# Issuing the attention bias loads of pairs 1 to 3 from SyncE, ahead of the pair's weight units

## The chip, the cores and the metric
The kernel runs on one core of a Trainium2 chip, as one program. The metric is the device time of the whole program in microseconds (us), the median of several executions. TensorE multiplies (PE in the profile; PEld is its weight load), VectorE is DVE, ScalarE is ACT, GpSimd is POOL, and SyncE (SP) only issues DMAs. ScalarE issues DMAs too; in the profile the rows marked SPq and ACTq are issues of these two engines' queues.

## The reference
One inference step of a one-layer hybrid encoder in float32: 1024 prompt frames and 8 streams of 16 frames (T = 1152 token columns) with D_MODEL = 1024. The layer is a half-step SwiGLU FFN, then two token mixers side by side (chunk-band softmax attention and a gated delta rule), cross-attention to 256 memory tokens, a second half-step FFN and a final norm. What matters here is mixer A:

```python
def band_attention_prompt(q, k, v, table):          # 8 heads x 64
    bias = rel_bias(table, qrel[:, None] - krel[None, :])
    ...
        sc = jnp.einsum('bqhd,bkhd->bhqk', qc, kb).astype(jnp.float32) * scale + bias
        p = jax.nn.softmax(sc, axis=-1).astype(v.dtype)
        return jnp.einsum('bhqk,bkhd->bqhd', p, vb)
```

Queries see a band of nine chunks of 64 frames. The 8 running streams do the same against 512 cached keys and their own 16. Each head has its own bias, a function of the relative distance.

## The kernel before
All products with weights are made as three float32r products (high by high, low by high, high by low): a weight unit of 128 x 1024 is loaded raw, GpSimd splits it into `w_hi` and `w_lo` (L133 and L136, in `split_units`), and TensorE runs jobs of 24 matmuls with it (three jobs to a unit, one for each third of the 1152 tokens). Three raw slots and three split slots form a ring, so that a unit's load waits until the unit before it in its slot has been split (`unit_split`), and a split waits until the products of the unit before it in its slot are done (`dense_done`) and its own unit has landed (`raw_landed`).

Mixer A works by pairs of heads, four pairs of them (`PAIRS = 4`, numbered 0 to 3). Pair 0 uses seven units, each later pair six: units 0 and 1 give q and k at the start of the pair (jobs 3 to 8), units 2 to 5 are filler work spread by a fixed plan between the attention steps; units 2 to 4 feed the convolution of mixer B, and unit 5 gives v of the next pair. A pair has nine attention steps (eight tiles of 128 queries and the streams): scores on TensorE, bias add and maximum on VectorE, exponential on ScalarE, normalisation on VectorE, transposes and the product with v on TensorE. Each product with v (`values`, L1431, for the streams L1418) raises the semaphore `valued`. It starts with one token, so that `valued.at(9 * i + 1)` is reached when all nine steps of the pairs before pair i have their values. After the ninth, TensorE runs only the last 16 filler matmuls of its pair before job 3 of the next one; job 3 needs that pair's unit 0 split (`job`, `n == 0`).

Every engine's instructions are in program order. TensorE, in a later pair: job 3, the transposes of v (`turn_v`, L1474 and L1477), jobs 4 to 7, the first scores, job 8, then the nine steps. There are two PSUM banks for jobs, so job 5 waits until ScalarE has evacuated job 3 (`take`, L1570). ScalarE, at the turn from one pair to the next: the last evacuation of v (L1528), the store of the pair's output (`ya`, L1657), `load_bias(i)` (L1557 to L1566), `next_conv` and `load_conv` (four DMA issues, L1545 to L1555), `take` of job 3, the copy of v, and the loads of the key and value caches (L1578), 2048 KB each.

`load_bias(i)` loads what pair i adds to its scores: for each of the two heads one window of 128 x 640 values (320 KB) and four copies of 16 x 528 values (33 KB), ten DMAs and 904 KB in all. VectorE waits for them (`a_loaded`) before it masks two corners of `bias` (L1726 and L1727) and adds it in its first step (L1740).

SyncE's queue in this stage is `load_units` (L71 to L108). It is called for pair 0 with one turn of seven units, and at its end loads the first three units of pair 1 ahead (L108). It is then called for pairs 1 to 3 with `turns = 3` and `turn = 6`: turn 0 (pair 1) issues its units 3 to 5; a hardware loop takes turn 1 (pair 2), and turn 2 (pair 3) is written out, both with units 0 to 5 (L82). `load_units` has a hook, `at_turn`, that is called once in each turn: in turn 0 behind the place of unit 0, in the later turns ahead of unit 0. The kernel before doesn't use it in this stage.

Of the kernel before, what the change touches and what calls it, by code (L numbers as in the profile page):

```python
# [17 lines left out]
DB, DS = 8, 16  # L18
# [5 lines left out]
HA, DHA, REACH, REL = 8, 64, 512, 128  # L24
HB, DHB, CW = 4, 128, 4
HX, DHX, NMEM = 4, 256, 256
WIN = REACH + P
# [27 lines left out]
def slot(j, turn):  # L55

    if (j, turn) == (4, 5):
        return 2
    return 1 if turn % RING == 1 and j == turn - 1 else j % RING


def sharing(j, turn):

    return [u for u in range(turn) if slot(u, turn) == slot(j, turn)]


def last_use(j, turn):

    same = sharing(j, turn)
    at = same.index(j)  # L70
    return (0, same[at - 1]) if at else (1, same[-1])  # L71


def load_units(sp, k, first, turns, turn, at_turn=None, then=None, apart=0, last=True):

    def one(i, j):
        back, last = last_use(j, turn)
        if not (isinstance(i, int) and i < back):  # L80
            sp.wait_ge(k.unit_split.sem, k.unit_split.at(turn * i + (last + 1 - turn * back)))
        sp.dma_start(k.w_raw[slot(j, turn)][:, :], k.units[k.host_unit(k.phase, i, first, j)])\  # L82
            .then_inc(k.raw_landed[slot(j, turn)].sem, 16)
    for j in range(turn):
        if j >= k.ahead:
            one(0, j)
        if at_turn and j == 0:
            at_turn(0)
        if then and j == RING - 1:
            then()  # L90
    if turns > 1:
        with sp.Fori(1, turns - apart) as i:
            if at_turn:
                at_turn(i)
            for j in range(turn):
                one(i, j)
    for i in range(turns - apart, turns):
        if at_turn:
            at_turn(i)
        for j in range(turn):  # L100
            one(i, j)
    if not last:
        return
    k.ahead = units_ahead(k)
    for j in range(k.ahead):
        users = sharing(j, turn) or [turn - 1]
        sp.wait_ge(k.unit_split.sem, k.unit_split.at(turn * (turns - 1) + users[-1] + 1))
        sp.dma_start(k.w_raw[j][:, :], k.units[k.host_unit(k.phase + 1, 0, first + turns * turn, j)]).then_inc(k.raw_landed[j].sem, 16)  # L108


def units_ahead(k):

    return min(RING, k.turn_sizes[k.phase + 1]) if k.phase + 1 < len(k.turn_sizes) else 0
# [59 lines left out]
def units_done(k, turns, turn):  # L173

    for u in range(turn):
        k.raw_landed[slot(u, turn)].base += 16 * turns
    for sig in (k.unit_hi, k.unit_split):
        sig.base += turns * turn
    k.next_unit += turns * turn
    k.phase += 1  # L180
# [1097 lines left out]
def attention_phase(nc, k, norm, decay, head, xh, xl, x, x_to, work):  # L1278
# [3 lines left out]
    def sb(name, shape):  # L1282
        t = nc.alloc_sbuf_tensor_at(name, shape, F32, offset=at[0])
        at[0] += (4 * int(np.prod(shape[1:])) + 31) // 32 * 32
        return t
# [7 lines left out]
    bias, bias_s = sb("a_bias", [P, 2, WIN]), sb("a_bias_s", [P, REACH + DS])  # L1293
# [6 lines left out]
    PAIRS, ND = HA // 2, 2  # L1300
# [8 lines left out]
    STEPS, SAMPLE, FULL = len(TILES), TILES.index(None), 4  # L1309
# [16 lines left out]
    shifted = k.bias_dram_flat[P - 1:P - 1 + P * (k.bias_pitch - 1)].rearrange("(q m) -> q m", q=P)[:, 0:HA * NBIAS]\  # L1326
        .rearrange("q (h m) -> h q m", h=HA)

    def window(t):

        n = min(5, t + 1)
        return t + 1 - n, n

    def keys_of(s):

        return 4 if TILES[s] is None else window(TILES[s])[1]

    def sync(sp):
        decay.load(sp)

        def store_x():
            sp.wait_ge(k.x_added.sem, k.x_added.at(NPS))
            for c in range(KD):
                sp.dma_start(x_to[c], x[:, c, :]).then_inc(k.loaded.sem, 16)

        load_units(sp, k, k.next_unit, 1, 7, then=store_x)
        units_done(k, 1, 7)
        load_units(sp, k, k.next_unit, PAIRS - 1, 6, apart=1)

    def gpsimd(pool):  # L1350
        split_units(pool, k, 1, (7, 8, 9, 12, 15, 18, 21), None, (0, 0, 0))
# [167 lines left out]
    def scalar(act):  # L1519
# [27 lines left out]
        def load_conv(i):  # L1547

            for dst, src in ((cst[:], k.conv_state[i]), (cw[:], k.conv_w[i])):
                act.dma_start(dst, src).then_inc(k.conv_loaded.sem, 16)  # L1550

        def next_conv(i):

            store_row(i, 2)
            act.dma_start(k.conv_out[i], cout[:]).then_inc(k.conv_stored.sem, 16)  # L1555

        def load_bias(i):  # L1557
            act.wait_ge(k.valued.sem, k.valued.at(STEPS * i + 1))
            loads = []
            for h in range(2):  # L1560
                loads.append((bias[:, h, :], shifted[2 * i + h][:, 0:WIN]))
                for b in range(4):
                    r = 32 * b + 16 * h
                    loads.append((bias_s[r:r + 16, :], shifted[2 * i + h][0:16, 0:REACH + DS]))
            for dst, src in loads:
                act.dma_start(dst, src).then_inc(k.a_loaded.sem, 16)  # L1566

        def take(i, g, u, n):
            act.wait_ge(k.dense_done.sem, k.dense_done.at(DONE * i + (g + 1)))
            act.activation((vt, q, kt)[u][:, n * THIRD:(n + 1) * THIRD], k.ps[g % ND][:, 0:THIRD], ACT.Copy,  # L1570
                           scale=DHA ** -0.5 if u == 1 else 1.0).then_inc(k.evacuated.sem, 1)

        def load_caches(i):

            act.wait_ge(norm.s.nscaled.sem, norm.s.nscaled.at(2 * norm.nb))
            act.wait_ge(k.loaded.sem, k.loaded.at(16 * KD))
            for dst, src in ((kc[:], k.k_cache[i]), (vc[:], k.v_cache[i])):
                act.dma_start(dst, src).then_inc(k.cache_loaded.sem, 16)  # L1578

        def copy_v(i):  # L1580
            act.wait_ge(k.v_turned.sem, k.v_turned.at(2 * i + 1))
            act.activation(vn[:].rearrange("p t c -> p (t c)"), psT[:, 0:8 * P], ACT.Copy).then_inc(k.vn_ready.sem, 1)
            act.wait_ge(k.v_turned.sem, k.v_turned.at(2 * i + 2))
            act.wait_ge(k.vns_clear.sem, k.vns_clear.at(1))
            act.activation(vns[0:DS].rearrange("p t c -> p (t c)"), psS[0:DS, 0:8 * P], ACT.Copy)\
                .then_inc(k.vn_ready.sem, 1)

        def exps(i, s, h):
            act.wait_ge(k.maxed.sem, k.maxed.at(2 * STEPS * i + 2 * s + h + 1))
            n = keys_of(s) * P if s != SAMPLE else REACH + DS  # L1590
            act.activation(sc[:, h, 0:n], sc[:, h, 0:n], ACT.Exp, bias=nmax[:, h:h + 1],
                           accum_out=rsum[:, h:h + 1]).then_inc(k.exped.sem, 1)
# [73 lines left out]
        for g in range(1, 9):  # L1666
            take(0, g, g % 3, g // 3)
            if g == 2:
                norm.upper(act, 2)
            if g == 5:  # L1670
                load_caches(0)
                load_conv(0)
            if g == 7:
                act.wait_ge(k.pre_pe.sem, k.pre_pe.at(1))
                load_bias(0)
        copy_v(0)
        pair(0)
        with act.Fori(1, PAIRS) as i:
            load_bias(i)
            next_conv(i - 1)  # L1680
            load_conv(i)
            for g in range(3, 9):
                if g == 3:
                    act.wait_ge(k.kv_stored.sem, k.kv_stored.at(32 * i + 32))
                if g == 8:
                    exps(i, 0, 0)
                    exps(i, 0, 1)
                take(i, g, g // 3, g % 3)
                if g == 3:
                    copy_v(i)  # L1690
                    load_caches(i)
            pair(i)
# [6 lines left out]
    def vector(dve):  # L1699
# [97 lines left out]
        decay.vector_behind(dve)  # L1797

    stage = Stage(k, sync, gpsimd, tensor, scalar, vector)
    units_done(k, 1, 7)  # L1800
    units_done(k, PAIRS - 1, 6)
# [1678 lines left out]
def hybrid_layer(nc, io):  # L3480
    with ExitStack() as ctx:
# [62 lines left out]
        ffn1 = ffn_phase(nc, k, "f1", None, x_early, xh1, xl1, work, sums_at, n2, BiasRows(nc, k, sums_at), memory_end)  # L3544
        decay, head = Decay(nc, k), FirstHead(nc, k, r2)
        attention = attention_phase(nc, k, n2, decay, head, xh1, xl1, x_early, k.x_dram, r2)
        branch = BranchA(nc, k, r2)
        delta = delta_phase(nc, k, decay, head, branch, xh1, xl1, r2)
# [107 lines left out]
```

## Time and profile before
| | us |
|---|---|
| median of 3 runs | 3281.96 (3279.01 to 3292.6) |
| the profiled execution | 3281.43 |
| its span, first to last instruction | 3279.6 |
| PE busy | 3155.4 |
| POOL, DVE and ACT busy | 1170.5, 1608.3 and 915.6 |

The profiled execution is 0.5 us from the median, so sums made on it can be set against the median as they are. Mixer A's pairs stand from about 925 us to 1374 us; its pairs 1, 2 and 3 begin at about 1036, 1148 and 1260 us. In a timeline row the first number is the start, the second the length of a merged piece, xN the number of instructions in it, and a bracket says how long the engine sat idle before the piece and what ended that time. Merged pieces of one engine's queue can span idle time.

### The profile page before, as it was taken

The numbers are of one execution on the slowest core, as the hardware profiler recorded it, in microseconds if no ns is written. First come the engines' busy times: TensorE is split into PE (matmuls) and PEld (weight loads), VectorE is DVE, ScalarE is ACT, GpSimd is POOL, SyncE is SP. The second block draws the span as 40 slices with busy tenths as digits, with TensorE's granted clock in tenths as the row PEclk, the third lists the DMA queues.
The fourth block names the chain that finished last, engine by engine and source line by source line (L and its number), as shares of the span: only waits on it lengthen the run. The fifth ranks groups of instructions, "written<-read, shape, count | busy, mean of one in ns | idle before, by whom it ended". The sixth has DMA issues, their size and how long they took to land.

```text
span 3279.6 us, 52298 instructions
## 1 busy us (share of the span) xinstructions
PE 3155.4 (96%) x19481; PEld 2997.6 (91%) x19481; DVE 1608.3 (49%) x2647; ACT 915.6 (28%) x1720; POOL 1170.5 (36%) x756
## 2 busy tenths in 40 slices
PE   6999999999999999999999999999899999999998
PEld 5999999999879888888897989988799999999997
DVE  6554445544645755653342466242328544455445
ACT  4122222112323333433433342132312222221123
POOL 5355555545412122111112134222123555555452
PEclk9999999999999999999999999999999999999999
DMA  5311111111233133211112145024311111111112
GB/s 190 132 39 39 51 38 58 45 38 38 102 115 135 53 131 125 82 67 45 65 50 81 37 166 176 26 92 168 135 33 39 39 39 51 38 58 45 38 39 77
DMA packets 92177, 247.48 MB, mean 75 GB/s; under 512 B 11536, under 2 KB 49168, under 8 KB 89360
## 3 DMA queue, kind: packets, MB, share of 16 engines
q1 hardware_dynamic: 52096, 157.24, 14.2%
q10 hardware_dynamic: 39952, 88.41, 7.5%
q8 instruction: 95, 1.56, 0.2%
q14 instruction: 34, 0.28, 0.0%
HBM read 197.87 MB, written 47.75 MB: 75 GB/s over the span
## 4 chain that ended last, share of the span: by engine, by line
PE 86%; DVE 7%; issue 3%; ACT 3%; DMA 1%; ACTq 1%; POOL 1%; SPq 0%; DVEq 0%; POOLq 0%
PE psum L168 58%; PE psum L264 13%; PE psum L2219 1%; DVE n_tmp L976 1%; PE psum L2155 1%; PE psum L1361 1%; PE psum L3216 1%; PE psum L1431 1%; PE psum L1406 1%; PE psum L3189 1%; DVE a_sc L1756 1%; PE psum L2169 1%; POOL w_lo L2719 1%; PE psum L2163 1%; PE psum L3195 1%
## 5 line engine op out<-in xcount | busy, mean ns | idle before, releaser
L133 POOL TENSOR_TENSOR w_hi<-w_raw,zero 128x1024 fp32r<-128x1024 f32 x79 | 158.2, 2003 | 1141.0 <-PE psum L264 783.6
L461 POOL TENSOR_TENSOR w_lo<-w_raw,w_hi 128x512 fp32r<-128x512 f32 x320 | 418.7, 1327 | 390.7 <-ACT w_hi L669 390.7
L168 PE MATMUL psum<-x_hi,w_hi 128*128 128x384 f32 x2288 | 465.3, 337 | 15.0 <-DVE x_lo L993 3.4
L168 PE MATMUL psum<-x_lo,w_hi 128*128 128x384 f32 x2288 | 463.7, 336 | 0.0
L168 PE MATMUL psum<-x_hi,w_lo 128*128 128x384 f32 x2288 | 459.6, 334 | 0.0
L168 PEld LDWEIGHTS psum<-x_hi,w_hi 128*128 128x128 f32 x2288 | 403.3, 189 | 23.0 <-issue 11.1
L168 PEld LDWEIGHTS psum<-x_lo,w_hi 128*128 128x128 f32 x2288 | 405.2, 189 | 2.2 <-issue 0.6
L168 PEld LDWEIGHTS psum<-x_hi,w_lo 128*128 128x128 f32 x2288 | 402.7, 188 | 0.0
L669 ACT ACTIVATE w_hi<-w_raw 128x512 fp32r<-128x512 f32 x320 | 192.6, 626 | 375.0 <-PE psum L168 309.5
L168 PE MATMUL psum<-f_h_hi,w_hi 128*128 128x384 f32 x1056 | 270.3, 336 | 5.2 <-DVE x_early L775 2.3
L168 PE MATMUL psum<-f_h_hi,w_lo 128*128 128x384 f32 x1056 | 268.6, 335 | 0.0
L168 PE MATMUL psum<-f_h_lo,w_hi 128*128 128x384 f32 x1056 | 268.6, 335 | 0.0
L264 PE MATMUL psum<-x_hi,w_hi 128*128 128x384 f32 x984 | 222.4, 349 | 6.6 <-ACT b_stash L2329 4.9
L264 PE MATMUL psum<-x_lo,w_hi 128*128 128x384 f32 x984 | 224.2, 351 | 0.0
L264 PE MATMUL psum<-x_hi,w_lo 128*128 128x384 f32 x984 | 214.2, 346 | 0.0
L136 POOL TENSOR_TENSOR w_lo<-w_raw,w_hi 128x1024 fp32r<-128x1024 f32 x79 | 201.1, 2545 | 6.2
L168 PEld LDWEIGHTS psum<-f_h_hi,w_hi 128*128 128x128 f32 x1056 | 190.7, 188 | 9.8 <-issue 3.9
L461 POOL TENSOR_TENSOR w_lo<-f_spare,w_hi 128x512 fp32r<-128x512 f32 x80 | 103.4, 1292 | 255.2 <-ACT w_hi L669 254.8
L168 PEld LDWEIGHTS psum<-f_h_hi,w_lo 128*128 128x128 f32 x1056 | 191.2, 188 | 0.0
L168 PEld LDWEIGHTS psum<-f_h_lo,w_hi 128*128 128x128 f32 x1056 | 191.0, 188 | 0.0
L168 PE MATMUL psum<-f_r,w_hi 128*128 128x384 f32 x960 | 185.7, 334 | 0.0
L775 DVE SCALAR_TENSOR_TENSOR x_late<-psum,x_late 128x384 f32<-128x384 f32 x264 | 141.3, 555 | 87.2 <-PE psum L168 87.2
(340 smaller groups left out, 4752.4 us busy)
## 6 DMA issues: line engine op xcount, KB each, us to landing
w_raw<-units SPq DMA_DIRECT2D x224, 512.0 KB, 3.9
gate_dram<-b_stash ACTq DMA_DIRECT2D x48, 192.0 KB, 1.9
e_gate<-gate_dram ACTq DMA_DIRECT2D x48, 192.0 KB, 2.8
a_kc<-k_cache ACTq DMA_DIRECT2D x4, 2048.0 KB, 8.1
a_vc<-v_cache ACTq DMA_DIRECT2D x4, 2048.0 KB, 12.5
proj_dram<-a_cv ACTq DMA_DIRECT2D x12, 576.0 KB, 2.8
b_pad<-proj_dram SPq DMA_DIRECT2D x12, 576.0 KB, 4.8
x_sk<-mem_k ACTq DMA_DIRECT2D x6, 1024.0 KB, 7.9
```

The lines of the kernel that those rows point to most:

```text
L133: pool.tensor_tensor(k.w_hi[s][:, :], k.w_raw[s][:, :], k.zero[:, 0:1].to_broadcast([P, D]), ALU.add)\
L136: pool.tensor_tensor(k.w_lo[s][:, :], k.w_raw[s][:, :], k.w_hi[s][:, :].bitcast(F32), ALU.subtract).then_inc(k.unit_split.sem, 1)
L168: mm = pe.matmul(out, wl if part == 2 else wh, (xl if part == 1 else xh)[:, n0:n1], start=(part == 0 and i == 0), stop=(part == 2 and i == ...
L264: mm = pe.matmul(k.ps[g % 2][:, 0:THIRD], w[:, c * P:(c + 1) * P], (xl if part == 1 else xh)[:, c, n * THIRD:(n + 1) * THIRD], start=(r == 0),
L461: pool.tensor_tensor(half(k.w_lo, h), raw_of(p, name), half(k.w_hi, h).bitcast(F32), ALU.subtract)\
L669: act.activation(half(k.w_hi, ITEM_HALF[m - 1]), raw_of(p, name), ACT.Copy).then_inc(k.unit_hi.sem, 1)
L775: dve.scalar_tensor_tensor(out=xs, in0=k.ps[(g - 12) % banks][:, 0:THIRD], scalar=0.5, in1=xs, op0=ALU.mult, op1=ALU.add).then_inc(k.x_add ...
L976: mm = dve.scalar_tensor_tensor(out=self.tmp[:, b, c, :], in0=self.x[:, c, self.cols(n)], scalar=self.gains[:, c:c + 1], in1=self.rinv[:, ...
L1361: return pe.matmul(psS[:, col:col + (b - a) * P], q[hp, t * P:(t + 1) * P], kt[hp, (k0 + a) * P:(k0 + b) * P], start=True, stop=True)
L1406: mm = pe.transpose(psT[:, j * P:(j + 1) * P], sc[:, h, j * P:(j + 1) * P], k.ident[:, :])
L1431: mm = pe.matmul(o[64 * h:64 * h + 64, :], vn[:, k0 + j, 64 * h:64 * h + 64], pt[:, h, j, :], start=(j == 0), stop=(j == n - 1), tile_posi ...
L1756: dve.tensor_scalar(sc[:, h, 0:n], sc[:, h, 0:n], rinv[:, h:h + 1], None, ALU.mult)\
```

## The change
`load_bias` becomes a function of the stage that takes the issuing engine. ScalarE still calls it for pair 0. For pairs 1 to 3 the call on ScalarE is taken out, and SyncE makes it from the hook of `load_units`, for pair i + 1 in turn i. The wait on `valued` goes with it. The ten transfers, their order and their semaphore are the same.

```diff
+    def load_bias(eng, i):
+        eng.wait_ge(k.valued.sem, k.valued.at(STEPS * i + 1))
+        for h in range(2):
+            eng.dma_start(bias[:, h, :], shifted[2 * i + h][:, 0:WIN]).then_inc(k.a_loaded.sem, 16)
+            for b in range(4):
+                r = 32 * b + 16 * h
+                eng.dma_start(bias_s[r:r + 16, :], shifted[2 * i + h][0:16, 0:REACH + DS]).then_inc(k.a_loaded.sem, 16)
+
     def sync(sp):
...
         load_units(sp, k, k.next_unit, 1, 7, then=store_x)
         units_done(k, 1, 7)
-        load_units(sp, k, k.next_unit, PAIRS - 1, 6, apart=1)
+        load_units(sp, k, k.next_unit, PAIRS - 1, 6, at_turn=lambda i: load_bias(sp, i + 1), apart=1)
...
-        def load_bias(i):
-            act.wait_ge(k.valued.sem, k.valued.at(STEPS * i + 1))
-            loads = []
...
-            for dst, src in loads:
-                act.dma_start(dst, src).then_inc(k.a_loaded.sem, 16)
...
                 act.wait_ge(k.pre_pe.sem, k.pre_pe.at(1))
-                load_bias(0)
+                load_bias(act, 0)
         copy_v(0)
         pair(0)
         with act.Fori(1, PAIRS) as i:
-            load_bias(i)
             next_conv(i - 1)
```

## Rows read from the trace of the kernel before

**Rows 1.** The page: busy time by engine, and the chain by engine.
```profile
PE 3155.4 (96%) x19481; PEld 2997.6 (91%) x19481; DVE 1608.3 (49%) x2647; ACT 915.6 (28%) x1720; POOL 1170.5 (36%) x756
...
PE 86%; DVE 7%; issue 3%; ACT 3%; DMA 1%; ACTq 1%; POOL 1%; SPq 0%; DVEq 0%; POOLq 0%
```

**Rows 2.** Timeline of PE from pair 1 into pair 2.
```profile
1143.88 1.31 PE L1431 MATMUL psum<-a_pt,a_vn 128*64 128x128 f32 x20
1145.12 1.68 PE L264 MATMUL psum<-x_lo,w_hi 128*128 128x384 f32 x8
1146.64 1.55 PE L264 MATMUL psum<-x_hi,w_lo 128*128 128x384 f32 x8
1148.03 1.55 PE L168 MATMUL psum<-x_hi,w_hi 128*128 128x384 f32 x8
...
1158.10 1.55 PE L168 MATMUL psum<-x_hi,w_hi 128*128 128x384 f32 x8
```

**Rows 3.** Timeline of ACT and its queue in the same stretch.
```profile
1149.33 0.37 ACTq L1566 DMA_DIRECT2D a_bias<-bias_dram  x1
...
1152.26 1.80 ACTq L1566 DMA_DIRECT2D a_bias_s<-bias_dram  x4
...
1157.06 0.49 ACT L1570 ACTIVATE a_q<-psum 128x384 f32<-128x384 f32 x1 [8.35 <-issue]
```

**Rows 4.** Busy time by windows (PE, PEld, DVE, ACT, POOL, clock, DMA share, GB/s).
```profile
1152.00:1156.00 4.00, 4.00 (x31) 3.81 (x30) 0.00 (x0) 0.00 (x0) 0.64 (x1) 1.00 0.87 274
1156.00:1160.00 4.00, 4.00 (x25) 4.00 (x24) 0.00 (x0) 2.66 (x4) 0.00 (x0) 1.00 0.88 264
1160.00:1170.00 10.00, 10.00 (x59) 10.00 (x59) 4.47 (x6) 0.98 (x2) 4.29 (x2) 1.00 0.96 401
```

**Rows 5.** Timeline of POOL: units 0, 1 and 2 of pair 2.
```profile
1105.46 1.89 POOL L133 TENSOR_TENSOR w_hi<-w_raw,zero 128x1024 fp32r<-128x1024 f32 x1 [17.76 <-PE psum L264]
...
1127.25 1.89 POOL L133 TENSOR_TENSOR w_hi<-w_raw,zero 128x1024 fp32r<-128x1024 f32 x1 [17.30 <-PE psum L264]
...
1148.27 1.89 POOL L133 TENSOR_TENSOR w_hi<-w_raw,zero 128x1024 fp32r<-128x1024 f32 x1 [16.54 <-PE psum L264]
1150.24 2.40 POOL L136 TENSOR_TENSOR w_lo<-w_raw,w_hi 128x1024 fp32r<-128x1024 f32 x1
```

**Rows 6.** SyncE's load of unit 0 of pair 2 (issue ns, start), its landing.
```profile
L82 SPq DMA_DIRECT2D w_raw<-units x1: 327/327/327, 1055.1 to 1055.1; - x1
DMA to landing us min/median/max: 6.5/6.5/6.5
```

**Rows 7.** A weight load beside bias loads, and landings of it (us).
```profile
L82 SPq DMA_DIRECT2D w_raw<-units x1: 328/328/328, 1152.7 to 1152.7; - x1
DMA to landing us min/median/max: 5.0/5.0/5.0
```

**Rows 8.** Landings: all of L82; two at 900 us; four bias copies from 1152.3 us.
```profile
DMA to landing us min/median/max: 3.3/4.3/14.3
...
DMA to landing us min/median/max: 7.9/7.9/8.0
...
DMA to landing us min/median/max: 2.7/3.7/4.3
```

**Rows 9.** PE after 8.78 us idle: half and full pace.
```profile
20.55 2.04 PE L168 MATMUL psum<-mem_hi,w_hi 128*128 128x256 f32 x8 [8.78 <-DVE mem_lo L993]
22.40 1.91 PE L168 MATMUL psum<-mem_lo,w_hi 128*128 128x256 f32 x8
24.10 1.91 PE L168 MATMUL psum<-mem_hi,w_lo 128*128 128x256 f32 x8
25.81 1.27 PE L168 MATMUL psum<-mem_hi,w_hi 128*128 128x256 f32 x8
...
28.84 1.12 PE L168 MATMUL psum<-mem_hi,w_hi 128*128 128x256 f32 x8
29.80 1.12 PE L168 MATMUL psum<-mem_lo,w_hi 128*128 128x256 f32 x8
```

**Rows 10.** Windows after 4.08 us idle, up to 1382.97 us (columns as in rows 4).
```profile
1384.00:1386.00 2.00, 2.00 (x7) 1.69 (x7) 0.21 (x1) 1.35 (x3) 0.00 (x0) 0.50 0.00 0
1386.00:1388.00 2.00, 2.00 (x6) 1.38 (x5) 1.36 (x2) 0.35 (x2) 0.00 (x0) 0.50 0.00 0
1388.00:1390.00 2.00, 2.00 (x11) 1.74 (x10) 0.56 (x1) 1.42 (x3) 0.00 (x0) 0.98 0.00 0
```

**Rows 11.** The turn into pair 1: last values (PE), unit 3's split (POOL).
```profile
1032.40 1.31 PE L1431 MATMUL psum<-a_pt,a_vn 128*64 128x128 f32 x20
...
1050.68 1.89 POOL L133 TENSOR_TENSOR w_hi<-w_raw,zero 128x1024 fp32r<-128x1024 f32 x1 [5.54 <-PE psum L168]
```

More of the change, by code:

```diff
@@ L1555, in next_conv @@
             act.dma_start(k.conv_out[i], cout[:]).then_inc(k.conv_stored.sem, 16)
-        def load_bias(i):
-            act.wait_ge(k.valued.sem, k.valued.at(STEPS * i + 1))
-            loads = []
[L1560 to L1564, printed above, removed]
-            for dst, src in loads:
-                act.dma_start(dst, src).then_inc(k.a_loaded.sem, 16)
         def take(i, g, u, n):
```

## The prediction
> **What bounds the kernel now.** I read the page first, then PE's timeline at the turn from pair 1 to pair 2, then the timelines of the engines that feed it. PE is busy for 96% of the span and holds 86% of the chain that ended last [rows 1]: this kernel is late by what makes PE idle, and by nothing else. At the turn of pair 2 the last product with v ends at 1143.88 + 1.31 = 1145.19 us, the last 16 filler matmuls start at 1145.12, and job 3 of pair 2, the first to use its unit 0, starts at 1148.03 with no idle time in its row [rows 2]. PE is then busy for 18.0 of 18.0 us [rows 4]. So there is nothing to win at a turn, and the reader should ask two things: was ScalarE, which is relieved, near to holding PE up; and how early must what stands behind the new wait on SyncE be?
>
> **What is removed: ten issues and a wait on ScalarE.** The ten issues run from 1149.33 to 1152.26 + 1.80 = 1154.06, 4.7 us [rows 3]. Behind them four other issues follow, and then the evacuation of job 3, from 1157.06 to 1157.55, for which ScalarE was late: its idle time before it ends by "issue", not by PE [rows 3]. Job 5, which takes the same bank, starts at 1158.10 [rows 2], directly behind job 4. The evacuation came 0.5 us before it was needed. Making it up to 4.7 us earlier gives PE nothing, since PE has no idle time there [rows 4]; what goes is a near miss. Value: 0 us, three times. Its end on the good side is also 0 by the windows, unless their records hide a gap; that is the last rival below. The wait on `valued` cost ScalarE nothing, since the same count is waited for ahead of its last output copy.
>
> The Trainium skill, page "DMA: Bandwidth & Descriptors", section "Issuing engines are not separate DMA queues", says that DMAs started by different engines run on the same 16 DMA engines, and that issuing from several saves only sequencer time. By that the bytes cost the same on either queue and the edit could win those 4.7 us of issue and no more; the rows above say even these are hidden.
>
> **What is added, pair 1: cover enough.** In turn 0 the hook stands behind the place of unit 0, whose load was made ahead, with those of units 1 and 2. Behind it are units 3 to 5. The wait is met when pair 0's values end, 1032.40 + 1.31 = 1033.7 us. Ten issues of 4.7 us bring unit 3 out at 1038.4 and, with 4 to 6.5 us of landing [rows 6], in at 1045 at the latest. Its split starts at 1050.68, held by PE's products, not by the load [rows 11]. 5.7 us or more of cover: 0 us.
>
> **What is added, pairs 2 and 3: no cover.** In turns 1 and 2 the hook stands ahead of unit 0. The wait for pair 2 needs all values of pair 1, so SyncE stands from the issue of pair 1's unit 5 until 1145.19, and all of pair 2's weight loads stand behind it. Before, unit 0 of pair 2 was issued at 1055.1 [rows 6], and split from 1105.46, a whole 42 us before its use; unit 1 from 1127.25 [rows 5]. POOL waits in order, so it now splits none of pair 2's units before unit 0 is in. The path from the last values to job 3:
> - SyncE wakes, 0.1 us (my allowance, from the step between the end of the values and the evacuation behind them);
> - ten bias issues. On ScalarE they took 4.7 us in the hardware loop [rows 3]. I take the same for SyncE: its weight issue is 0.33 us [rows 6] and the first bias issue of ScalarE 0.37, so 3.3 us is the least for ten; 5.5 us is the most that I allow, should the queue stop for a moment. Unit 0 is out at 1150.0 us;
> - its landing. Alone a weight load of 512 KB lands in 3.3 us at best; beside bias loads on the other queue it took 5.0 [rows 7], beside the caches 6.5 [rows 6], beside many stores 7.9 to 8.0 [rows 8]. Here 904 KB of bias go out just ahead of it, the last copies of which land in up to 4.3 us [rows 8], and ScalarE's stores of 576 KB twice beside it. I take 5.2, near the row that is likest: in at 1155.2. The ends are 3.3 and 8.0;
> - the split, 1148.27 to 1150.24 + 2.40 = 1152.64, is 4.4 us [rows 5], and a semaphore at both ends, 0.2 us: done at 1159.8.
>
> Job 3 would start at 1159.8 and not at 1148.03: **11.8 us idle**, ends 8.5 us (0.1 + 3.3 + 3.3 + 4.6, less the 2.84 from the values' end to job 3) and 15.4 us (0.1 + 5.5 + 8.0 + 4.6 - 2.84).
>
> The Trainium skill, page "DMA: Bandwidth & Descriptors", section "Queues, rings and completion order", says that descriptors of one queue are consumed in ring order and that the queues take turns. So unit 0 would stand behind all bias bytes that are not yet through. Had none gone by its issue, 904 KB at the 401 GB/s of the third window [rows 4] would add 2.3 us to the 3.3 of a lone load, 5.6 in all; since most have gone by then, I stay at 5.2. No row before shows both on one queue.
>
> Units 1 and 2 follow 4.4 us apart on POOL, unit 1 is wanted 14 us after job 3's start: hidden. The same goes for units 3 to 5, issued as their slots come free. Pair 3 is the same again.
>
> **The clock.** A PE that has stood idle comes back slower in this trace. After 8.78 us idle, eight matmuls of 256 columns took 1.70 us (22.40 to 24.10, 24.10 to 25.81) where later they take 0.96 (28.84 to 29.80): 24 of them in 5.26 us instead of 2.88, 2.4 us lost [rows 9]. After 4.08 us idle the granted clock was 0.50, which is 1.2 GHz, until 1388, against full 2.4 GHz behind it [rows 10]; PE had restarted at 1382.97, so 5.0 us ran at half pace: 2.5 us lost. I take 2.5 us a turn, ends 2.0 and 3.0. Nothing later in a pair gives time back: its other steps wait for each other as before.
>
> **The sum.** 2 x (11.8 + 2.5) = 28.6 us on 3281.43: **3310.0 us**, 0.87% slower. With all low ends 2 x (8.5 + 2.0) = 21.0, 3302; with all high ends 2 x (15.4 + 3.0) = 36.8, 3318. Runs of before lie from 3 us below to 11 us above their median, so I add a little at both ends: own range 3300 to 3320.
>
> **The rivals.**
> - *Loads held longer.* Unit 0 shares the DMA engines with units 1 and 2 right behind it, with ScalarE's stores (now up to 5 us earlier) and with short packets of the convolution's state, and lands in 10 to 14 us; one of all 59 loads took 14.3 [rows 8]. For: several queues at work. Against: where unit and bias loads were side by side it was 5.0 [rows 7]. Time: 2 x (0.1 + 4.7 + 12 + 4.6 - 2.84 + 2.5) = 42, 3323.
> - *One turn alone is held.* The hook stands ahead of unit 0 in turns 1 and 2, but the second is written out and the first is in a hardware loop; should one of them not block the loads, the cost is one time 14.3: 3295.7, inside 0.5% of before. Against: both call the same hook first.
> - *Nothing is held: the change doesn't do what it says.* If the wait were met early, SyncE would pass it, and the loads come as before: 3282. Against: the token and nine steps a pair put it at the last values, and ScalarE waited for the same count.
> - *The other side: ScalarE binds at the turns.* The evacuation of job 3 comes 0.5 us before job 5 [rows 2, 3]. If PE's modelled ends hid a wait there, up to 4.7 us would be freed at each of three turns, 14.1: 3267 with the loads' wait hidden too. It decides only if that gap exceeds what the held unit costs, more than 8 us a turn at the least. Against: 18.0 busy us of 18.0 [rows 4].
>
> **How the numbers follow.** Forecast 0.84; loads held longer 0.07; one turn 0.04; nothing held 0.03; the other side 0.02. A measurement of this kernel can tell 0.5%, 16.4 us, from no change, so slower begins at 3298.4. Slower: 0.84 + 0.07 and nothing of the rest, 0.91. Same: 0.04 + 0.03 = 0.07. Faster: 0.02. The range 3300 to 3321 takes the forecast's own range and a little of the first rival.
>
> **What would show it.** In the trace after: SPq rows of L82 for pairs 2 and 3 right behind ten bias issues, none between pair 1's unit 5 and the last values; a first split of pair 2 some 10 us behind these values, with the idle time of POOL before it ended by the DMA; job 3 of pairs 2 and 3 with 10 to 13 us idle, released by `w_lo`; a granted clock of 0.50 behind it for some 5 us; no such gap at pair 1; `a_q` of job 3 on ACT released by PE. The prediction is wrong if unit 0 of pair 2 is issued before the last values of pair 1, if its landing is beyond 8 us, or if PE fills the gap.

## The result, and the profile after

| | before | after |
|---|---|---|
| median, us | 3281.96 | 3311.26 |
| lowest to highest of 5 runs | 3279.01 to 3292.6 | 3307.77 to 3314.14 |
| span of the profiled execution | 3279.6 | 3306.9 |

The changed kernel is slower: ratio 1.0083, 95% interval 1.0071 to 1.0095. The forecast was 3310.0 us (range 3300 to 3321) and slower. The spans differ by 27.3 us.

The page after; to be set beside [rows 1]. PE did the same work in 2 us more and fell from 96% to 95% of a longer span. The group of L168 that had 15.0 us of idle time ahead of it on the page before now has 42.5, and the releaser named is new (the last two lines: before, after).
```profile
PE 3157.6 (95%) x19481; PEld 3001.5 (91%) x19481; DVE 1595.9 (48%) x2647; ACT 916.3 (28%) x1720; POOL 1170.9 (35%) x756
...
L168 PE MATMUL psum<-x_hi,w_hi 128*128 128x384 f32 x2288 | 465.3, 337 | 15.0 <-DVE x_lo L993 3.4
...
L168 PE MATMUL psum<-x_hi,w_hi 128*128 128x384 f32 x2288 | 466.8, 338 | 42.5 <-POOL w_lo L136 28.0
```

Which waits these are is in the list of PE's waits, asked for mixer A's stretch alone (total us, times, longest); the last line is of the kernel before.
```profile
PE psum L168 <- POOL w_lo L136: 27.3, 2, 14.5
...
PE psum L1414 <- DVE a_sc L1752: 2.8, 4, 1.2
...
PE psum L1406 <- DVE a_sc L1756: 6.1, 10, 1.2
```
Two waits, 27.3 us, at the turns into pairs 2 and 3. The other two lines are a wait that got shorter: before, PE waited ten times and 6.1 us for `a_sc`, after it four times and 2.8 us. Nothing in the prediction spoke of it.

The turn into pair 2, SyncE's queue, POOL and PE of the kernel after (start, length, as in [rows 2, 3, 5]):
```profile
1142.07 0.33 SPq L1341 DMA_DIRECT2D a_bias<-bias_dram  x1
1142.44 1.82 SPq L1344 DMA_DIRECT2D a_bias_s<-bias_dram  x4
1144.31 0.42 SPq L1341 DMA_DIRECT2D a_bias<-bias_dram  x1
1144.77 2.59 SPq L1344 DMA_DIRECT2D a_bias_s<-bias_dram  x4
1147.40 19.28 SPq L82 DMA_DIRECT2D w_raw<-units  x6
```
```profile
1153.42 1.89 POOL L133 TENSOR_TENSOR w_hi<-w_raw,zero 128x1024 fp32r<-128x1024 f32 x1 [66.55 <-DMA w_raw<-units]
1155.39 2.34 POOL L136 TENSOR_TENSOR w_lo<-w_raw,w_hi 128x1024 fp32r<-128x1024 f32 x1
```
```profile
1140.72 1.31 PE L1439 MATMUL psum<-a_pt,a_vn 128*64 128x128 f32 x20
...
1157.86 2.92 PE L168 MATMUL psum<-x_hi,w_hi 128*128 128x384 f32 x8 [12.82 <-POOL w_lo L136]
1160.58 2.21 PE L168 MATMUL psum<-x_lo,w_hi 128*128 128x384 f32 x8
1162.62 1.55 PE L168 MATMUL psum<-x_hi,w_lo 128*128 128x384 f32 x8
1164.02 1.03 PE L1482 MATMUL psum<-ident,a_v 128*128 128x128 f32 x8
...
1284.01 2.92 PE L168 MATMUL psum<-x_hi,w_hi 128*128 128x384 f32 x8 [14.50 <-POOL w_lo L136]
```
Read it as one chain: the last values end at 1142.03; SyncE's first issue is at 1142.07 and the last of the ten ends at 1147.36; the first weight load goes out at 1147.40 and lands 5.9 us later (7.7 at the next turn); POOL, which had stood for 66.55 us until that DMA, starts at 1153.42 and is done at 1157.73; job 3 starts at 1157.86. Job 3 then takes until 1164.02, 6.2 us. In the kernel before it took 4.2, from 1148.03 [rows 2] to the first transpose of v behind it. That row, and the rows of unit 0's two loads in the changed kernel (issue in ns, landing in us):
```profile
1152.19 1.03 PE L1474 MATMUL psum<-ident,a_v 128*128 128x128 f32 x8
```
```profile
L82 SPq DMA_DIRECT2D w_raw<-units x1: 1163/1163/1163, 1147.4 to 1147.4; - x1
DMA to landing us min/median/max: 5.9/5.9/5.9
...
L82 SPq DMA_DIRECT2D w_raw<-units x1: 1116/1116/1116, 1271.8 to 1271.8; - x1
DMA to landing us min/median/max: 7.7/7.7/7.7
```

ScalarE's evacuation of job 3 is now released by PE, not late by "issue" as in [rows 3]:
```profile
1164.21 0.49 ACT L1567 ACTIVATE a_q<-psum 128x384 f32<-128x384 f32 x1 [18.65 <-PE psum L168]
```

### The profile page after: what moved, and what is told of

It reads as the page before. It is cut to its first block, busy times and chain, and to the rows that moved or that the text cites. A ratio compares the mean times of both kernels' runs of the same rounds, so it can differ in the third digit from the quotient of the medians.

```text
span 3306.9 us, 52262 instructions
## 1 busy us (share of the span) xinstructions
PE 3157.6 (95%) x19481; PEld 3001.5 (91%) x19481; DVE 1595.9 (48%) x2647; ACT 916.3 (28%) x1720; POOL 1170.9 (35%) x756
## 4 chain that ended last, share of the span: by engine, by line
PE 84%; DVE 6%; issue 5%; ACT 3%; POOL 1%; DMA 1%; ACTq 1%; SPq 0%; DVEq 0%; POOLq 0%
PE psum L168 58%; PE psum L264 12%; PE psum L2215 1%; DVE n_tmp L976 1%; PE psum L2151 1%; PE psum L3212 1%; PE psum L1369 1%; PE psum L3185 1%; PE psum L1414 1%; PE psum L1439 1%; PE psum L2165 1%; PE psum L2159 1%; PE psum L3191 1%; POOL w_lo L2715 1%; PE psum L933 0%
## 5 line engine op out<-in xcount | busy, mean ns | idle before, releaser
L168 PE MATMUL psum<-x_hi,w_hi 128*128 128x384 f32 x2288 | 466.8, 338 | 42.5 <-POOL w_lo L136 28.0
L168 PE MATMUL psum<-x_lo,w_hi 128*128 128x384 f32 x2288 | 465.0, 337 | 0.0
L168 PE MATMUL psum<-x_hi,w_lo 128*128 128x384 f32 x2288 | 459.6, 334 | 0.0
L168 PEld LDWEIGHTS psum<-x_hi,w_hi 128*128 128x128 f32 x2288 | 404.3, 189 | 51.1 <-issue 39.3
L168 PEld LDWEIGHTS psum<-x_lo,w_hi 128*128 128x128 f32 x2288 | 406.7, 190 | 2.2 <-issue 0.6
L168 PEld LDWEIGHTS psum<-x_hi,w_lo 128*128 128x128 f32 x2288 | 402.8, 188 | 0.0
L168 PE MATMUL psum<-f_h_hi,w_hi 128*128 128x384 f32 x1056 | 270.3, 336 | 5.2 <-DVE x_early L775 2.3
L168 PE MATMUL psum<-f_h_hi,w_lo 128*128 128x384 f32 x1056 | 268.6, 335 | 0.0
L168 PE MATMUL psum<-f_h_lo,w_hi 128*128 128x384 f32 x1056 | 268.6, 335 | 0.0
L168 PEld LDWEIGHTS psum<-f_h_hi,w_hi 128*128 128x128 f32 x1056 | 190.7, 188 | 9.8 <-issue 3.9
L168 PEld LDWEIGHTS psum<-f_h_hi,w_lo 128*128 128x128 f32 x1056 | 191.2, 188 | 0.0
L168 PEld LDWEIGHTS psum<-f_h_lo,w_hi 128*128 128x128 f32 x1056 | 191.2, 188 | 0.0
L168 PE MATMUL psum<-f_r,w_hi 128*128 128x384 f32 x960 | 185.7, 334 | 0.0
```

What stands on the lines that cost most here:

```text
L168: mm = pe.matmul(out, wl if part == 2 else wh, (xl if part == 1 else xh)[:, n0:n1], start=(part == 0 and i == 0), stop=(part == 2 and i == ...
```

## The experiments

Each kernel was run beside the kernel before on its chip (medians there 3282.6 to 3284.1 us), with a profile. x6, x7 and x9 were run once each, so only their spans and traces are read. The length of a pair is read from the start of the last product with v of one pair to that of the next; for pairs 1, 2 and 3:

| kernel | pair 1 | pair 2 | pair 3 | sum | against before |
|---|---|---|---|---|---|
| before | 111.48 | 111.86 | 111.65 | 334.99 | |
| after | 109.15 | 124.47 | 128.42 | 362.04 | +27.0 |
| x1, behind unit 2 | 111.46 | 111.84 | 111.65 | 334.95 | 0.0 |
| x2, wait only | 109.15 | 117.65 | 118.81 | 345.61 | +10.6 |
| x3, POOL held | 109.16 | 113.57 | 115.73 | 338.46 | +3.5 |
| x4, off the normalisation | 109.30 | 109.65 | 109.65 | 328.60 | -6.4 |
| x5, behind unit 0 | 109.73 | 110.54 | 111.66 | 331.93 | -3.1 |
| x6, 100 transposes added in each pair | 120.14 | 126.07 | 126.05 | 372.26 | +37.3 |
| x7, small windows | 109.17 | 124.35 | 125.57 | 359.09 | +24.1 |
| x8, x4 and x1 together | 109.29 | 109.65 | 109.63 | 328.57 | -6.4 |
| x9, convolution later | 109.18 | 123.62 | 125.42 | 358.22 | +23.2 |

Each row comes from one profiled execution. Drifts elsewhere in the program are not in it: the product from which pair 1 is counted starts anywhere from 1031.55 to 1034.88 us in these traces, though nothing ahead of it was changed.

### x1: the same call, behind unit 2
```diff
             for j in range(turn):
                 one(i, j)
+                if at_turn and j == behind:
+                    at_turn(i)
...
-        load_units(sp, k, k.next_unit, PAIRS - 1, 6, at_turn=lambda i: load_bias(sp, i + 1), apart=1)
+        load_units(sp, k, k.next_unit, PAIRS - 1, 6, at_turn=lambda i: load_bias(sp, i + 1), apart=1, behind=2)
```
(and no call ahead of unit 0 in turns 1 and 2; turn 0, with its units 0 to 2 loaded ahead, is as in the changed kernel)

> The changed kernel with the bias call moved in SyncE's queue: behind the place of unit 2 in every turn, not ahead of unit 0. ScalarE is relieved as in the changed kernel. Theory A (the whole loss is that units 0 to 2 of pairs 2 and 3 stand behind the wait and the ten issues; ScalarE's relief is worth nothing): no idle of PE at a turn, granted clock 1.00 there, 3282 us, within 4 us of before. Rival B (ScalarE's issue time does bind somewhere, and the stall hid the gain): 3268 to 3275. Rival C (what costs is the bias on SyncE's queue, wherever it stands): still above 3295.

Measured: 3285.4 us, ratio 1.0008 (0.9999 to 1.0017). In its trace SyncE makes the ten issues from 1144.37 on, as late as in the changed kernel; units 0 to 2 had been loaded long before. PE is busy for 10.00 of 10.00 us at the turn, at full clock:
```profile
1145.00:1155.00 10.00, 10.00 (x66) 9.81 (x65) 2.25 (x6) 2.90 (x4) 4.29 (x2) 1.00 0.89 288
```
So the ten issues on SyncE cost nothing by themselves, and neither does PE gain by ScalarE's losing them. ScalarE's evacuation of job 3 is now released by PE, as soon as the job is done, and yet PE's pairs have the lengths of before to 0.02 us:
```profile
1151.71 0.49 ACT L1571 ACTIVATE a_q<-psum 128x384 f32<-128x384 f32 x1 [3.86 <-PE psum L172]
```
Theory A holds, B and C fall.

### x2: only the wait is moved
```diff
-        load_units(sp, k, k.next_unit, PAIRS - 1, 6, apart=1)
+        load_units(sp, k, k.next_unit, PAIRS - 1, 6,
+                   at_turn=lambda i: sp.wait_ge(k.valued.sem, k.valued.at(STEPS * (i + 1) + 1)), apart=1)
```


> The kernel before, ScalarE still makes all bias issues, but SyncE makes the wait for the last values of a pair ahead of the next pair's unit 0. Theory A (the idle of a turn is wait to landing to split; the ten issues are 5.3 us of it and lengthen the landing from about 4 to 5.9 and 7.7 us): idle of PE at turns 2 and 3 of 0.1 + 4.3 + 0.1 + 4.3 - 2.8 = 6 us each and not 12.8 and 14.5, with 2.0 us of clock each, less the 2.3 us that each of pairs 1 and 2 got shorter by: 3282 + 2 x 5.7 = 3293 us. Rival B (the issues and their transfers make the whole loss, a waiting queue costs nothing): under 3285.

Measured: 3292.93 us, ratio 1.0031 (1.0017 to 1.0044). PE's two waits:
```profile
1152.29 2.92 PE L168 MATMUL psum<-x_hi,w_hi 128*128 128x384 f32 x8 [5.87 <-POOL w_lo L136]
...
1269.39 2.92 PE L168 MATMUL psum<-x_hi,w_hi 128*128 128x384 f32 x8 [5.31 <-POOL w_lo L136]
```
5.9 and 5.3 us, where 6 were expected; unit 0 landed in 4.3 us at the first and 3.8 at the second. A wait that costs ScalarE nothing, since it stands there behind the same count, costs 10.6 us on SyncE. Of the 27.3 us of idle time in the changed kernel, 11.2 are the wait with the landing and split behind it, and the other 16.1 come with the ten issues standing in between: 5.3 and 5.2 us of issue, and the rest longer landings (5.9 and 7.7 us).

### x3: GpSimd alone is held
```diff
+        def hold(i, j):
+            if j == 0 and not (isinstance(i, int) and i in (0, PAIRS - 1)):
+                pool.wait_ge(k.valued.sem, k.valued.at(STEPS * (i + 1) + 1))
```
(`split_units` calls it ahead of its own waits)

> The kernel before with SyncE and ScalarE as they were; only GpSimd waits for the last values of a pair before it splits unit 0 of the next one (pairs 2 and 3). The unit has landed long before. Theory D (pairs 1 and 2 of the changed kernel were 2.3 us shorter because GpSimd's splits of units 0 and 1 of the next pair no longer ran beside VectorE's normalisation, which takes 1.7 to 2.5 us beside a split and 0.55 us alone): the normalisations of steps 5 and 7 of pairs 1 and 2 are all at 0.55 us, these pairs 2.3 us shorter, and PE idle at turns 2 and 3 for 0.1 + 4.4 + 0.1 - 2.8 = 1.8 us each with no fall of the clock: 3281 us in all. Rival E (the pairs were shorter because of what left ScalarE or SyncE, not because of the splits): normalisations as before, no shorter pairs, 3285.5 us.

Measured: 3284.54 us, ratio 0.9998 (0.9989 to 1.0008). This run is about the time that came back. It has to be read from the pairs: the sum in the table is 3.5 us up, while the interval of the medians ends at 2.6. Pair 1 lasts 109.16 us instead of 111.48, though SyncE and ScalarE do what they did before: what shortened pair 1 of the changed kernel by 2.3 us was that no split ran in its steps 5 and 7. The kernel before, step 5 of pair 1, VectorE and, last, POOL:
```profile
1105.96 1.74 DVE L1756 TENSOR_SCALAR a_sc<-a_sc,a_rinv 128x640 f32<-128x640 f32 x1
...
1107.81 2.49 DVE L1756 TENSOR_SCALAR a_sc<-a_sc,a_rinv 128x640 f32<-128x640 f32 x1
...
1107.43 2.52 POOL L136 TENSOR_TENSOR w_lo<-w_raw,w_hi 128x1024 fp32r<-128x1024 f32 x1
```
and the same step of the changed kernel, with no split beside it:
```profile
1105.14 0.56 DVE L1752 TENSOR_SCALAR a_sc<-a_sc,a_rinv 128x640 f32<-128x640 f32 x1
...
1106.22 0.55 DVE L1752 TENSOR_SCALAR a_sc<-a_sc,a_rinv 128x640 f32<-128x640 f32 x1
```
Theory D holds. One number of its expectation was wrong: the granted clock did fall, during job 3 and behind only 2.3 us of idle time, and job 3 took 5.9 us (1147.74 to 1153.60) and not 4.2. That is 1.7 us a turn, and with it the sum comes near: 2 x (2.2 + 1.7) - 2 x 2.3 = 3.2, measured +3.5.
```profile
1147.74 2.22 PE L172 MATMUL psum<-x_hi,w_hi 128*128 128x384 f32 x8 [2.26 <-POOL w_lo L138]
```
```profile
1148.00:1150.00 2.00, 2.00 (x9) 2.00 (x9) 2.00 (x2) 0.00 (x0) 2.00 (x1) 0.65 0.90 227
1150.00:1152.00 2.00, 2.00 (x7) 2.00 (x7) 2.00 (x3) 0.00 (x0) 1.92 (x2) 0.50 1.04 344
```

### x4: the splits moved off the normalisation
```diff
-        split_units(pool, k, PAIRS - 1, (3, 6, 9, 12, 15, 18), None, (-9, 0, -3))
+
+        def hold(i, j):
+            if j < 2 and not (isinstance(i, int) and i == 0):
+                pool.wait_ge(k.normed.sem, k.normed.at(2 * STEPS * i + (12, 16)[j]))
+
+        split_units(pool, k, PAIRS - 1, (3, 6, 9, 12, 15, 18), None, (-9, 0, -3), hold=hold)
+        pool.wait_ge(k.normed.sem, k.normed.at(2 * STEPS * (PAIRS - 1) + 16))
```


> The kernel before with two holds on GpSimd in pairs 1 to 3: it splits unit 0 of the next pair (or stage) only when both normalisations of step 5 are done, and unit 1 only when those of step 7 are. Both are wanted 20 us or more later. Theory D (split and normalisation slow each other where they coincide, and PE waits for the normalisation): 2.3 us less in each of pairs 1 to 3, 3275 us (0.2% faster). Rival E (the slow normalisations have another cause, or PE finds another wait behind): 3282 us. Rival F (the splits, now beside the convolution's taps, slow those down and these hold something up): 3284 or more.

Measured: 3277.09 us, ratio 0.9983 (0.9974 to 0.9992) over 11 runs, against 3283.65 before. Each pair is 2.0 to 2.2 us shorter, 6.4 in all. What is slow now is a tap of the convolution, for which nobody waits (step 5 of pair 1):
```profile
1107.97 0.55 DVE L1766 TENSOR_SCALAR a_sc<-a_sc,a_rinv 128x640 f32<-128x640 f32 x1
...
1109.05 0.55 DVE L1766 TENSOR_SCALAR a_sc<-a_sc,a_rinv 128x640 f32<-128x640 f32 x1
...
1112.22 2.38 DVE L1781 TENSOR_SCALAR a_cv<-a_stash,a_cw 128x128 f32<-128x128 f32 x1
```
It beats both kernels. The gain, 0.17%, is below the 0.5% named in the prediction as what a usual measurement tells from no change, but its interval over 11 runs leaves out 1.

### x5: the same call, behind unit 0
```diff
+                if at_turn and j == behind:
+                    at_turn(i)
...
-        load_units(sp, k, k.next_unit, PAIRS - 1, 6, at_turn=lambda i: load_bias(sp, i + 1), apart=1)
+        load_units(sp, k, k.next_unit, PAIRS - 1, 6, at_turn=lambda i: load_bias(sp, i + 1), apart=1, behind=0)
```


> The changed kernel with the bias call behind the place of unit 0 in every turn: unit 0 of pairs 2 and 3 is loaded ahead again, units 1 and 2 still stand behind the wait and the ten issues. Theory A: unit 1 is out 5.4 us behind the last values, lands 6 to 7.7 us later and is split 4.4 us after that, 15.9 to 17.6 us in all, and job 6 wants it 2.8 + 14.3 = 17.1 us behind them: no idle of PE at turn 2, at most 0.5 us at turn 3, no fall of the clock. Theory D: unit 0's split runs beside step 5's normalisation again (its 1.7 and 2.5 us come back), unit 1's no longer beside step 7's: 1.6 us less in each of pairs 1 and 2. In all 3279 us. Rival: any load of the next pair behind the wait costs its time, another 10 us a turn, over 3295.

Measured: 3280.66 us, ratio 0.9997 (0.9988 to 1.0007). At turn 2 unit 1 was just in time, 0.18 us late, and at turn 3 in time:
```profile
1163.34 1.67 PE L172 MATMUL psum<-x_hi,w_hi 128*128 128x384 f32 x8 [0.18 <-POOL w_lo L140]
```
The pairs are 3.1 us shorter in all, as theory D has it for one of two slow steps. So one load of 512 KB, unit 0's, ahead of the wait and not behind it makes the difference between +27.0 us and -3.1. The median alone would not have shown the 3.1 us.

### x6: PE kept busy in the idle time
```diff
         with pe.Fori(1, PAIRS) as i:
+            for d in range(100):
+                pe.transpose(psT[:, 0:P], k.ident[:, :], k.ident[:, :])
```


> The changed kernel with 100 transposes of the unit matrix, 0.109 us each, into a free bank ahead of job 3 in pairs 1 to 3; their result is overwritten. In pairs 2 and 3 they stand in the idle time of the turn, in pair 1 there is none, so they cost 10.9 us there. Theory A (2.0 us a turn of the loss are the lower clock behind the idle time): granted clock 1.00 in job 3 of pairs 2 and 3, its 24 matmuls in 4.16 us and not 6.16, the rest of the idle time 2 and 3.6 us; a span of 3306.9 + 10.9 - 4.0 = 3314 us. Rival (job 3 is slow for another reason, the traffic or the first use of the unit): job 3 stays at 6.2 us, span 3318 us.

Measured: span 3316.9 us, 3 us above the expectation and 1 us below the rival's 3318, so the span decides nothing and the rows of the two turns have to. At turn 3 job 3 ran at full pace behind the transposes and 2.27 us of remaining idle time, as theory A has it:
```profile
1284.63 11.11 PE L1519 MATMUL psum<-ident 128*128 128x128 f32 x100 [0.73 <-issue]
...
1298.01 1.68 PE L168 MATMUL psum<-x_hi,w_hi 128*128 128x384 f32 x8 [2.27 <-POOL w_lo L136]
1299.53 1.55 PE L168 MATMUL psum<-x_lo,w_hi 128*128 128x384 f32 x8
```
At turn 2, behind the same transposes and 2.35 us, the clock fell all the same, from 1174 on, and job 3 took 5.9 us:
```profile
1172.53 1.91 PE L168 MATMUL psum<-x_hi,w_hi 128*128 128x384 f32 x8 [2.35 <-POOL w_lo L136]
...
1174.00:1176.00 2.00, 2.00 (x8) 2.00 (x7) 0.00 (x0) 0.00 (x0) 1.92 (x2) 0.50 0.50 201
```
And SyncE's ten issues took 7.9 us there (1154.87 to 1162.77) and 7.7 at turn 3, not 5.3; why, with only PE's work changed, stays open. The 3 us above the expectation are these two: the clock that was not kept at turn 2, 1.7 us, and a path from the last values to job 3 that was 1.9 us longer there and 0.4 shorter at turn 3. That job 3 was slow because of the clock is shown by turn 3 and by the windows of x3. That two idle times of 2.3 us end differently is shown, its reason is not.

### x7: small bias windows
```diff
-            eng.dma_start(bias[:, h, :], shifted[2 * i + h][:, 0:WIN]).then_inc(k.a_loaded.sem, 16)
+            rows = P if isinstance(i, int) and i == 0 else 16
+            eng.dma_start(bias[0:rows, h, :], shifted[2 * i + h][0:rows, 0:WIN]).then_inc(k.a_loaded.sem, 16)
```


> The changed kernel, but the two bias windows of pairs 1 to 3 are loaded for 16 of 128 partitions only (40 KB each and not 320), so the scores of these pairs use stale bias on the others; ten issues as before. If the bytes ahead of unit 0 in SyncE's queue lengthen its landing (5.9 and 7.7 us in the changed kernel, 4.4 where only the wait was moved), it lands in 4.5 to 5 us, idle at the turns 11.5 and 12 us, span 3303 us. Rival (ScalarE's stores and the short packets beside it lengthen it): landing as before, span 3307 us.

Measured: span 3305.6 us, idle 12.7 and 12.3 us. Unit 0's two loads:
```profile
L82 SPq DMA_DIRECT2D w_raw<-units x1: 421/421/421, 1149.5 to 1149.5; - x1
DMA to landing us min/median/max: 6.2/6.2/6.2
...
L82 SPq DMA_DIRECT2D w_raw<-units x1: 420/420/420, 1273.8 to 1273.8; - x1
DMA to landing us min/median/max: 5.8/5.8/5.8
```
It landed in 6.2 us (5.9 in the changed kernel) and 5.8 (7.7). The 560 KB taken away did not shorten the first landing. The second is 1.9 us shorter, which this single profile can't put down to the bytes. The expectation of 4.5 to 5 us is refuted. The bytes did show in the issues: the last four bias copies took 2.2 us at both turns, and 2.5 to 2.6 in the changed kernel. Unit 0's own issue fell from 1.16 and 1.12 us to 0.42, but x9 has 0.44 and 0.45 with the windows whole, so that is not the bytes alone.

### x9: the convolution's transfers later
```diff
         with act.Fori(1, PAIRS) as i:
-            next_conv(i - 1)
-            load_conv(i)
...
                     copy_v(i)
+                    next_conv(i - 1)
+                    load_conv(i)
```


> The changed kernel with ScalarE's four issues of the convolution (a store of 576 KB, a store of 40 KB and two loads in short packets) behind the evacuation of job 3 in each turn and not ahead of it, so that only the store of the pair's output is beside SyncE's ten issues and unit 0. If these four lengthen what stands on SyncE's queue (the last four bias copies took 2.6 us there and not 1.8, the issue of unit 0 1.16 us and not 0.33, its landing 5.9 and 7.7 us and not the 4.3 of the run with the wait alone): the ten issues take 4.6 us, unit 0 issues in 0.33 and lands in 4.4 to 5 us, idle of PE 10.8 to 11.3 us at both turns, span 3302 us. Rival (units 1 and 2 right behind it and the bias ahead of it are what lengthen it): issues and landing as in the changed kernel, span 3307 us.

Measured: span 3304.1 us. Unit 0's issue and landing at the two turns:
```profile
L82 SPq DMA_DIRECT2D w_raw<-units x1: 440/440/440, 1147.9 to 1147.9; - x1
DMA to landing us min/median/max: 4.4/4.4/4.4
...
L82 SPq DMA_DIRECT2D w_raw<-units x1: 453/453/453, 1271.4 to 1271.4; - x1
DMA to landing us min/median/max: 4.6/4.6/4.6
```
Landings near those of x2 (4.3 and 3.8), and 11.3 us idle at each turn, 22.6 in all for 27.3. With the four transfers of the convolution moved away the landings are 1.5 and 3.1 us shorter; in the changed kernel ScalarE, rid of the bias, issued these four right beside unit 0. That they lengthen the landing is what the one edit shows. By how much is less certain, since these are single profiles: with the four beside it unit 0 took 5.9 and 7.7 us in the changed kernel, 6.2 and 5.8 in x7, and 5.2 and 4.9 in x6, where all four had been issued before it. The span is 2 us above the expected 3302; job 3 took 6.8 and 6.5 us in this run, more clock lost than in the changed kernel. One part is refuted: the last four bias copies still took 2.56 us to issue, not 1.8.

### x8: the holds of x4 with SyncE's issues behind unit 2
```diff
+        load_units(sp, k, k.next_unit, PAIRS - 1, 6, at_turn=lambda i: load_bias(sp, i + 1), apart=1, behind=2)
...
+        split_units(pool, k, PAIRS - 1, (3, 6, 9, 12, 15, 18), None, (-9, 0, -3), hold=hold)
+        pool.wait_ge(k.normed.sem, k.normed.at(2 * STEPS * (PAIRS - 1) + 16))
```


> The two holds on GpSimd of the kernel that splits off the normalisation, together with SyncE's bias loads behind unit 2. Theory: ScalarE's relief is worth nothing with or without the slow normalisations, so the time is that of the holds alone, 0.998 of before, 3277 us. Rival (with the normalisations fast, ScalarE's issues at the turn are next): 0.996 or less, 3271 us.

Measured: 3276.96 us, ratio 0.9984 (0.9975 to 0.9993) over 11 runs: the holds' gain and nothing more. ScalarE's relief is worth nothing in this form either.

## Why the prediction was right, step by step

- **ScalarE's relief: 0 us.** Right. Shown by x1 (0.0 us over three pairs) and x8. The near miss read off [rows 2, 3] was just that.
- **Pair 1: cover enough.** Right. Unit 3 was split at 1049.86, held by PE, as in [rows 11]; no wait of PE for a split at that turn.
- **The wait ahead of unit 0: all of the loss.** Right in place and mechanism: x1 and x5 take it away by moving one call behind one or three loads.
- **Ten issues, 4.7 us.** Measured 5.3 and 5.2. The first five go as on ScalarE [rows 3]; the last four copies take 2.5 to 2.6 us, not 1.8. Inside the bounds given. With small windows they take 2.2 (x7), so some 0.3 us go with the windows' bytes; what the rest is stays open. It is not the convolution's transfers (x9).
- **Landing of unit 0, 5.2 us.** Measured 5.9 and 7.7, inside the bounds of 3.3 and 8.0. The term that was sized too small. The row taken for it [rows 7] had bias loads beside it; what counted were ScalarE's four transfers (x9). The bytes ahead in the same queue were not what lengthened the first landing (6.2 us with 560 KB fewer of them, x7); for the second x7 leaves it open. The prediction had weighed these bytes by the Trainium skill, page "DMA: Bandwidth & Descriptors", section "Queues, rings and completion order", that descriptors of one queue are consumed in ring order; the first landing does not show a cost of that kind here.
- **Split and semaphores, 4.6 us.** 1153.42 to 1157.73 is 4.3, and 0.1 to PE.
- **Idle time, 11.8 us a turn.** Measured 12.8 and 14.5: 3.7 us more in all than forecast.
- **The clock, 2.5 us a turn.** Measured 2.0 and 2.1 (job 3 in 6.2 us, not 4.2); 1.2 GHz until 1162, then 2.4 GHz:
```profile
1158.00:1160.00 2.00, 2.00 (x7) 2.00 (x8) 0.00 (x0) 0.00 (x0) 1.92 (x2) 0.50 0.59 141
1160.00:1162.00 2.00, 2.00 (x8) 2.00 (x7) 0.00 (x0) 0.00 (x0) 2.00 (x2) 0.50 0.30 121
1162.00:1164.00 2.00, 2.00 (x13) 1.98 (x12) 0.00 (x0) 0.00 (x0) 1.92 (x3) 1.00 0.33 92
```
- **"Nothing later in a pair gives time back."** Wrong, and the term was put at nothing. Pair 1 gave back 2.3 us and pair 2, with its idle time and clock taken off, 2.2, 4.5 in all, since the splits of the next pair's units 0 and 1 left their steps 5 and 7 (x3, x4). Both ends of it were in the trace before: the splits of [rows 5] at 1105.46 and 1127.25, and normalisations of 1.74 and 2.49 us where others take 0.55.

The measured sum of mixer A: 27.3 (idle) + 4.1 (clock) - 4.5 (given back) = 26.9, against +27.0 in the pairs' lengths and 27.3 in the spans. The forecast had 23.6 + 5.0 = 28.6. So 3.7 us too little idle time was more than balanced by 0.9 too much for the clock and 4.5 overlooked. The mechanism of the loss was foreseen; that the number came out within 1.3 us is luck, since two errors of about 4 us each cancelled. It is 1.3 us below the median, and 1.3 us above the profiled execution (3308.72), on whose predecessor the sum was made.

## What to carry to other kernels

A wait that is free on one engine is not free on another: before moving an instruction with its wait, list what is queued behind it there and how early that has to be. A DMA queue that prefetches must have the prefetches ahead of a late wait; here one load on the right side of it is worth 30 us. And when an engine's work moves in time, look for what it ran beside as well as for who waits for it.

## What the runs showed of the hardware that was not expected

- VectorE's normalisation, SBUF to SBUF in float32, takes 0.55 us, but 1.74 and 2.49 us when it starts under a split of GpSimd, and ends 0.35 us behind the split each time (1107.70 behind 1107.35; 1110.30 behind 1109.95). The maximum that runs into the start of the first split keeps its 0.82 us. x3 and x4 show that this cost PE 2.0 to 2.3 us a pair. The Trainium skill, page "SBUF — State Buffer", section "Who interferes with whom", states this as a port pair that VectorE in certain modes and GpSimd hold exclusively for a whole instruction, the other blocked. The trace agrees: 0.35 us behind the split's end in both rows.
- The granted clock fell to 0.50 (1.2 GHz) during the first job behind 2.26 us of idle time (x3), and in x6 once behind 2.35 us and once not behind 2.27. In x6 PE had also stood for 1.24 us ahead of the transposes at the turn where it fell, and for 0.73 at the other; whether that matters was not tested.
- Four transfers on ScalarE's queue (576, 40.5, 36 and 6 KB) lengthened the landing of a 512 KB load on SyncE's queue from 4.4 and 4.6 us to 5.9 and 7.7 (x9 against the changed kernel, one profile each; 6.2 and 5.8 in x7).
